# Down projection's changes of chunk: the low parts of two of the seven new input blocks made by GpSimd instead of VectorE

## What is computed

```
u, v = split(h @ w_up)                 # 544 x 2048 by 2048 x 11264
f    = (gelu(causal_dwconv(u)) * v) @ w_down    # 544 x 5632 by 5632 x 2048
y    = layer_norm(ALPHA * h + f)
```

## Time and profile before

| | us |
|---|---|
| median of 3 runs (2959.11 to 2973.03) | 2962.35 |
| the profiled execution's own time | 2959.66 |
| its span in the profile | 2957.9 |
| TensorE busy (matmul) | 2793.3 (94%) |
| VectorE busy | 2284.4 (77%) |
| ScalarE busy | 1374.4 (46%) |
| GpSimd busy | 360.0 (12%) |

### The profile page before, as it was taken

How to read it: one execution, slowest core, us unless ns; L and a number is a source line. 1 busy time by engine, 2 the same in 40 slices (tenths; PEclk the granted TensorE clock), 3 DMA queues, 4 the chain that set the end, 5 groups by cost and what they waited for, 6 DMA issues and landing times.

```text
span 2957.9 us, 55336 instructions
## 1 busy us (share of the span) xinstructions
PE 2793.3 (94%) x22589; PEld 2669.5 (90%) x22589; DVE 2284.4 (77%) x3567; ACT 1374.4 (46%) x2351; POOL 360.0 (12%) x332
## 2 busy tenths in 40 slices
PE   8999999989988869989989999999999999999996
PEld 8999999988877658889989999999999999999996
DVE  6656877877667677755588888888888888888898
ACT  5434545546545544432254444444444453435354
POOL 0010000013370215124330000000000000000012
PEclk9999999999999989999999999999999999999998
DMA  7564444458722883563354434444444464534343
GB/s 221 178 205 106 116 124 122 114 162 285 260 92 96 339 245 107 151 177 86 86 172 117 136 110 132 124 128 119 123 134 118 128 202 153 162 111 149 119 124 118
DMA packets 521473, 440.12 MB, mean 149 GB/s; under 512 B 36264, under 2 KB 476767, under 8 KB 515147
## 3 DMA queue, kind: packets, MB, share of 16 engines
q1 hardware_dynamic: 456662, 300.70, 35.4%
q0 software_dynamic: 20288, 82.91, 7.7%
q10 hardware_dynamic: 44272, 52.98, 5.3%
HBM read 378.31 MB, written 66.55 MB: 150 GB/s over the span
## 4 chain that ended last, share of the span: by engine, by line
PE 49%; DVE 5%; issue 1%; POOL 1%; ACT 1%; DMA 0%; DVEq 0%; ACTq 0%; POOLq 0%
PE i L3293 42%; PE i L140 7%; DVE f_half L3799 1%; DVE x_blocks L3837 1%; POOL x_blocks L3241 1%; DVE h_rows L3832 0%; DVE y_rows L3930 0%; DVE w_ring L3788 0%; DVE x_blocks L3765 0%; PE i L3302 0%; DVE y_rows L3923 0%; DMA x_blocks<-s_blk 0%; DVE f_sum L3792 0%; DVE ln_parts L3843 0%; DVE f_sum L3781 0%
## 5 line engine op out<-in xcount | busy, mean ns | idle before, releaser
L3293 PE MATMUL i<-x_blocks,f_half 128*128 128x272 f32 x10752 | 1361.1, 288 | 22.5 <-DVE h_rows L3832 10.9
L3293 PEld LDWEIGHTS i<-x_blocks,f_half 128*128 128x128 f32 x10752 | 1351.7, 189 | 27.5 <-DVE x_blocks L3837 11.8
L570 PE MATMUL a<-xb_in,w_half 128*128 128x272 f32 x4200 | 548.0, 292 | 9.2 <-DVE w_half L972 5.3
L570 PEld LDWEIGHTS a<-xb_in,w_half 128*128 128x128 f32 x4200 | 537.5, 190 | 18.2 <-issue 7.2
L3516 ACT CAST f_half<-w_ring 128x1024 fp32r<-128x1024 f32 (+2 forms) x370 | 346.2, 936 | 407.1 <-PE i L3293 352.3
L3799 DVE TENSOR_TENSOR f_half<-w_ring,f_half 128x1024 fp32r<-128x1024 f32 (+2 forms) x362 | 393.4, 1087 | 80.6 <-ACT f_half L3516 78.1
L3799 DVE TENSOR_TENSOR f_half<-f_sum,f_half 128x1024 fp32r<-128x1024 f32 (+2 forms) x148 | 159.5, 1078 | 82.0 <-ACT f_half L3516 81.8
L972 DVE TENSOR_TENSOR w_half<-w_ring,w_half 128x1024 fp32r<-128x1024 f32 x129 | 157.5, 1222 | 81.3 <-ACT w_half L708 81.0
L3516 ACT CAST f_half<-f_sum 128x1024 fp32r<-128x1024 f32 (+2 forms) x148 | 138.8, 938 | 151.4 <-PE i L3293 151.4
L3253 POOL TENSOR_TENSOR f_half<-w_ring,f_half 128x512 fp32r<-128x512 f32 x8 | 13.8, 1725 | 1396.7 <-ACT f_half L3516 1396.7
L708 ACT CAST w_half<-w_ring 128x1024 fp32r<-128x1024 f32 x125 | 131.3, 1051 | 108.7 <-PE a L570 105.8
(11 more groups left out here) (569 smaller groups left out, 4109.5 us busy)
## 6 DMA issues: line engine op xcount, KB each, us to landing
w_ring<-in_ffn_w_up_dram SPq DMA_DIRECT2D x88, 1024.0 KB
w_ring<-in_w_in_dram SPq DMA_DIRECT2D x52, 1024.0 KB, 8.8
w_ring<-in_ffn_w_down_dram SPq DMA_DIRECT2D x24, 1536.0 KB, 7.1
w_ring<-in_w_o_dram SPq DMA_DIRECT2D x16, 1024.0 KB
x_blocks<-s_blk ACTq DMA_DIRECT2D x17, 816.0 KB, 5.1
s_proj<-st ACTq DMA_DIRECT2D x48, 272.0 KB, 3.1
s_blk<-x_sums ACTq DMA_DIRECT2D x22, 544.0 KB, 6.6
kv_ring<-in_cmp_w_dram SPq DMA_DIRECT2D x16, 512.0 KB, 7.2
```

Of the source, the lines that this page charges most:

```text
L570: last = nc.tensor.matmul(ps[bank][:, 0:HT2], half(q, w)[:, k], XB[v[j]][:, k], start=j in (0, 1, 3) and k == 0 and i == 0, stop=k == HK - ...
L3293: last = nc.tensor.matmul(ps[bank][:, 0:HT2], half(e, j, wl_)[:, s], XB[:, x0 + s, xl_, BLK_OF[j]], start=start and s == 0 and i == 0, sto ...
```

## The change

`X_POOL = (3, 5)`: the low parts of X3 and X5 are made by GpSimd at all four changes of chunk, with the same instruction (`tensor_tensor`, subtract, same sizes). They are counted on the semaphore `ll` (in use before for the first input blocks) in place of `xq`, and `x_wait` chooses between the two. VectorE's list loses these eight instructions, GpSimd's gains them.

```diff
+        X_POOL = (3, 5)
+        X_N, n_x = {}, [0, 0]
+        for c in range(4):
+            for b in range(7):
+                n_x[b in X_POOL] += 1
+                X_N[c, b] = n_x[b in X_POOL]
...
+            def x_wait(eng, c, b):
+                if b in X_POOL:
+                    eng.wait_ge(ll, KT + X_N[c, b])
+                else:
+                    eng.wait_ge(xq, X_N[c, b])
...
                             if c:
-                                sp.wait_ge(xq, 7 * c + b + 1)
+                                x_wait(sp, c, b)
...
-                sp.wait_ge(xq, 28)
+                x_wait(sp, 3, 5)
+                x_wait(sp, 3, 6)
...
                 for e in range(NP):
                     for j in range(7):
+                        for xc_, b in X_PREP.get((e, j), ()):
+                            if b in X_POOL:
+                                gp.wait_ge(xhq, 7 * xc_ + b + 1)
+                                nc.gpsimd.tensor_tensor(block_of(xc_, b, 1), raw_block(xc_, b), block_of(xc_, b, 0).bitcast(F32), ALU.subtract).then_inc(ll, 1)
                         if on_pool(e, j):
...
                         if first:
-                            pe.wait_ge(xq, 7 * c + j + 1)
+                            x_wait(pe, c, j)
...
                         for xc_, b in X_PREP.get((e, n), ()):
-                            x_low(xc_, b)
+                            if b not in X_POOL:
+                                x_low(xc_, b)
```

## The result

| | before | after |
|---|---|---|
| median, us | 2962.91 (4 runs: the three above and one more) | 2977.81 (4 runs, 2976.62 to 2978.46) |
| profiled execution's span | 2957.9 | 2976.0 |
| VectorE busy | 2284.4 | 2293.1 |
| GpSimd busy | 360.0 | 387.6 |

What follows compares the result with a forecast made beforehand. VectorE's work was taken to set TensorE's pauses at the changes of chunk, beside the clock. The terms 3.4 + 4.3 + 4.3 + 4.1 = 16.1 us gave 2978 us, range 2968 to 2987.

Steps and rivals of the forecast that it cites:

- The mechanism: VectorE instructions with two SBUF inputs wait for the whole of a GpSimd instruction that reads SBUF; add_down is free.
- GpSimd's instruction: GpSimd's subtraction at the changes of chunk: an estimate of 3.8 us for 1632 columns, 2.6 for 1088.
- Second change: Sum 2 held, new pause before P1, P2 without pause, P6 2.7 us later with a second slow stretch: +4.3 us.
- The rival of a missed 0.2 us: GpSimd late at sum 2, gets in at the next add_down, P1 not late: +2.5 us, total 2975; chance 0.22.
- First change: VectorE held twice for 3.4 us and spared 1.77 twice; P6 3.3 to 4.3 us later, keeping its slow stretch: +3.4.
- Chunk 3: P3's weight block waits behind X5 in GpSimd's list; P6 3.1 us later, 4.7 with a second slow stretch: +4.1.
- the slow stretches: TensorE at 1.2 instead of 2.4 GHz behind pauses, some 1.6 us each; a second one at second and third change.
- No mutual waiting: At all changes only GpSimd's length counts: -2.0, -1.9, -1.9, and +3 in chunk 3; sum -2.8, 2960; chance 0.07.
- VectorE doesn't catch up in the pair behind: One more pause of 1 to 3 us with a slow stretch at two or three changes: 20 to 26 us, 2985; chance 0.23.
- How GpSimd gets in: At the changes, a waiting GpSimd instruction gets in at VectorE's next add_down, which has one input in PSUM.

Runs made afterwards that it cites:

- e2: Changed kernel with one GpSimd memset in place of each subtraction, low parts of X3 and X5 left out; 2959.03 us against 2964.52 before, ratio 0.9985.
- e6: Changed kernel with P3's weight block ahead of X5 in GpSimd's list in chunk 3; 2975.79 us against 2962.91 before, ratio 1.0042.
- e9: Changed kernel with one memset per block instead of subtracting, and P3's weight block ahead of X5 in chunk 3; 2945.81 us against 2956.35 before, ratio 0.9964.
- e7: Kernel before, with X4's preparation on VectorE one step later, behind the first add_down, for c = 1 to 3; 2961.32 us against 2962.91, ratio 0.9993.
- e3: Changed kernel with GpSimd making the low part of X3 alone, X5 back on VectorE; 2970.39 us against 2964.52 before, ratio 1.0019.

## Why the prediction was right, and where it wasn't

**The mechanism** was right and is shown: VectorE held (4.31 us for 0.95, and 0.95 beside 4.50 us of memsets, which read nothing). Of the Trainium skill's rule in "SBUF — State Buffer", section "Who interferes with whom", that the contention is with a GpSimd instruction that reads SBUF and not with one that only writes it, these two runs show both halves. The VectorE instructions of the earlier trace rows are additions and not the subtractions that the text calls them; they have two inputs in SBUF all the same, and the reading stands.

**GpSimd's instruction** was estimated at 3.8 us and took 3.67 where nothing delayed it, 2.5 for 2.6 in chunk 3.

**Second change.** New pause before P1: 3.7 forecast, 3.42 measured. The 3.7 was rounded down twice on its way (P0's end is 2572.20 - 3.44 - 2.25 = 2566.5, not 2566, so its own replay gives 3.1 to 3.2); P1's start was right: 2569.6 less X0's cast at 2550.14 is 19.5 us, and 2577.09 - 2557.59 = 19.5. P6's delay against X0's cast: 2.7 forecast; 2593.95 - 2557.59 = 36.4 us against 2583.50 - 2550.14 = 33.4 before, so 3.0. At the third change it was 2.9. The rival of a missed 0.2 us is out at the second change: a lead of 0.17 us was enough. At the third, GpSimd was released 0.25 us behind sum 2's start instead and got in one instruction later, before f_half (4.43 us); P1's pause was 3.54 all the same.

**First change.** P6 came 4.2 us later (2457.72 - 2420.91 = 36.8 against 32.65), within the forecast 3.3 to 4.3; the two holds were 3.52 and 3.46 us (5.37 for 1.85, 3.71 for 0.25), forecast 3.4 each.

**Chunk 3.** P6 came 3.2 us later (2862.43 - 2834.40 = 28.0 against 24.9), forecast 3.1 without a second slow stretch; P3 waited for the block as forecast. What wasn't seen is that the holds and the order are each enough alone (e2, e6, e9).

**What was mis-sized: the slow stretches.** The sum had one more of 1.6 us behind P6 at the second and third change and a share of one in chunk 3; only the third change had it. The windows of the changed kernel behind P6 at the second, then at the third change (us, busy us of PE, PEld, DVE, ACT, POOL, granted clock, DMA):

```profile
2596.00:2599.00 3.00, 3.00 (x26) 3.00 (x25) 2.81 (x4) 1.10 (x2) 0.00 (x0) 1.00 0.76 238
```

```profile
2732.30:2734.30 2.00, 1.99 (x10) 2.00 (x11) 2.00 (x4) 0.00 (x0) 0.00 (x0) 0.59 1.05 368
```

The pauses are 2.51 and 2.49 us. So 4.3 + 4.3 became 3.0 + 4.5; at the first change P6 had no slow stretch (96 matmuls in 12.48 us) where before had one, which e7 shows to come and go by itself, and 3.4 became 2.9; 4.1 became 3.2. The sum is 13.5 instead of 16.1 us. That the median of 2977.81 lies on the forecast 2978 is in part luck: the one execution of after with a profile among them also came 4.6 us late to the first change, ahead of any changed instruction (for the others nothing shows it), and the ratios put the change at 12 to 13 us, just inside the 0.5% that the text gave as its bound, where the forecast lay just outside.

**The rivals.** "No mutual waiting" gave -2.0, -1.9, -1.9 and +3; with three memsets, which are that case, the parts are -2.4, -2.2, -2.2 and +3.7. "VectorE doesn't catch up in the pair behind" didn't come: behind P6 TensorE has no pause. How GpSimd gets in was put too narrowly, see below.

## What to carry to other kernels

An instruction moved from a busy VectorE to an idle GpSimd is paid for with up to GpSimd's duration, not with nothing, if VectorE's work next to it takes two inputs from SBUF: here VectorE was held 2.3 to 3.5 us beside each instruction of some 3.7 us, against 1.8 saved. A memset, which reads nothing, did not hold it. Even then the place in GpSimd's own list counts: in chunk 3 it cost 2 us. Ask of a saved pause or a slow stretch whether the next product waits for the same engine anyway, and of a wait with two causes whether taking one away can show at all.

## What the runs showed of the hardware

- A waiting GpSimd instruction does not need VectorE to come to an instruction with one SBUF input. It got in between two back-to-back VectorE instructions with two SBUF inputs: released at 2430.29 during f_half, ahead of X2 at 2430.62 (5.37 us), and ahead of f_half at 2711.43. Before, released at 2834.39, it had let X4 pass at 2834.86; what made the difference there stays open.
- GpSimd's read of one input holds VectorE as one of two does (2.18 us for 0.95 beside a copy of 1.55); a memset doesn't (0.95 beside three of 4.50 us together).
- The length of a pause does not settle TensorE's clock. Behind the same pause of 2.01 us, 60 matmuls took 9.31 us before and 7.75 in e7; behind 2.51 us the clock stayed at 1.00 in the changed kernel, behind 2.44 at the same place in e6 90 matmuls took 12.98 instead of 11.48. Nor is a pause under 2 us safe, as e7's text supposed: in e3, at the third change, the clock still reads 0.50 behind a pause of 0.72 us that follows one of 3.52 and 18 matmuls.
